# Two-layer streaming encoder on one core: four attention buffers and an even fill, modulation by row products on VectorE, first loads by channel tile

## The chip, the cores and the metric

The kernel runs on one core of one Trainium2 chip. A core has a matrix engine (TensorE, called PE in the profile, with its weight loads as PEld), three elementwise engines (VectorE = DVE, ScalarE = ACT, GpSimd = POOL) and a queue engine (SyncE = SP). SP and ACT start the DMAs. The engines run their own instruction streams in order and meet only at semaphores. The metric is the device time of one execution in microseconds (us), as the median of several runs.

## The reference

The model is a two-layer trunk over 1024 tokens of width 1024, all in fp32. Layer 0 uses forgetting attention (16 heads of 64, causal, with a bias from a cumulative log forget gate), layer 1 a sliding-window attention over a shared K/V. Both have a gated feed-forward part (FFN) with a causal convolution of three taps over 2 x 2816 channels. What the change is about is the modulation: every norm is scaled and shifted, and every branch is gated, by vectors that come from one product of a conditioning vector with a large matrix.

```python
def _modulate(x, g, shift, scale):
    return _rmsnorm(x, g) * (1.0 + scale[:, None, :]) + shift[:, None, :]

c_act = jax.nn.silu(c)                          # 1 x 1024
for l in range(DEPTH):                          # DEPTH = 2
    mod = c_act @ ada_w[l] + ada_b[l]           # 1024 x 6144 per layer
    sh1, sc1, g1, sh2, sc2, g2 = jnp.split(mod, 6, axis=-1)
    if l == N_A:                                # N_A = 1: own product of 1024 x 2048
        k_band, v_band = _shared_kv(x, c_act, kv_norm_g, kv_ada_w, kv_ada_b, kv_w)
    h = _modulate(x, norm1_g[l], sh1, sc1)
    y = forgetting attention (l = 0) or sliding-window attention (l = 1) of h
    x = x + g1[:, None, :] * y
    h = _modulate(x, norm2_g[l], sh2, sc2)
    x = x + g2[:, None, :] * _conv_ffn(h, ...)
return _rmsnorm(x, final_g)
```

In all 112 blocks of 128 modulation values are needed: 16 ahead of the first projection (shift and scale of the first norm), 32 more of layer 0 (the two gates, shift and scale of its second norm), and 64 for layer 1 and the shared K/V.

## The kernel before

Activations lie transposed: channels on the 128 partitions in 8 channel tiles, tokens along the free dimension. Every fp32 product is made of three matmuls with a high part (rounded to fp32r) and a low part (the rest) of each operand; ACT writes the high parts and DVE or POOL subtracts to get the low ones. The weights come through one stream of tiles of 512 KB: SP loads them into two raw buffers (`w_raw`), POOL (and ACT in the FFN) splits them into `w_spl`.

The stages in order of time are these. First X and the modulation weights are loaded, PE sums squares for the norm (line 638), and DVE multiplies each 128 x 512 piece of modulation weights by a scalar per partition and adds it to an accumulator (`ada_steps`, lines 1619 and 1622). PE sums the accumulator over the partitions with one-column matmuls (`ada_cols`, line 631), and DVE adds the bias (line 1633). After the last of these the norm is applied tile by tile: `scaled` on DVE (line 1601), two passes on ACT (lines 1126 and 1129), and `low` on DVE (line 1606); PE makes V and the gate from each tile as it comes (line 664).

Layer 0's attention runs in 4 groups of 4 heads. A head has 12 tasks, each a key block of 128 against up to 512 queries (`TASKS`). In each task slot T of a group PE issues the scores of task T (lines 775, 785, 788), then the value products of task T - `LAG` (lines 810 to 812), then the score maxima for the next head (line 749, counts per slot in `MAX_T`), then steps of the next Q and K projection as filling (line 614, counts per slot in `FILL_1` and `FILL_2`). ACT takes the exponential into `PF` (line 1187) and the high part into `PH` (line 1194), and DVE makes the low part `PL` (line 1726), which the value products wait for. There are three such buffers, and the exponential of a task waits until the value products of the task three before are done. The order of all this is written out by these tables; nothing is scheduled by a tool. Between the tasks DVE also does a modulation step of 128 x 256 in eight of a head's 12 slots, and PE the one-column matmuls in the twelfth.

After the last head PE does the output projection in 8 tiles m (line 614); DVE adds each to X with the gate (line 1833), and the product of tile m waits for the sum of tile m - 2. ACT squares the new X for the next norm.

The FFN (lines 882 for all its matmuls) works on 22 pairs of channel tiles; from the third pair on, the up projection is a seven-product scheme (products A11, A12, S1, S2, S4, A22, S3 of 12 matmuls each) followed by 48 matmuls of the down projection. ACT copies a product out (`u_copy_of`, line 1375), DVE adds such copies (line 1884), makes the convolution taps (lines 1861, 1864) and adds the down projection to X (line 1891). In the 16 pairs 3 to 18 of layer 0 the modulation of layer 1 and of the shared K/V is made beside it: 16 steps of 128 x 256 a pair on DVE from four buffers, with the DMAs issued by ACT between its other work (line 1411), and one-column matmuls on PE after A11 and after S4. The FFN of layer 1 is the same without any modulation.

## Time and profile before

| | |
|---|---|
| median of 3 runs | 2567.02 us (2564.18 to 2570.03) |
| the profiled execution | 2563.79 us |
| its span, first to last instruction | 2562.0 us |
| PE busy | 2371.5 us, 93% of the span, 11208 matmuls |
| DVE / ACT / POOL busy | 1583.9 / 1150.2 / 1133.5 us |
| mean granted TensorE clock | 0.96 of full |
| moved by DMA | 205.41 MB, mean 80 GB/s |

The 1.8 us between the profiled time and its span lie outside the instructions. The profiled execution is 3.2 us under the median of the three runs. PE is busy nearly all the time, but a busy microsecond at half the clock does half the work, so idle time and granted clock are read together, stage by stage.

### The profile page before, as it was taken

The page shows a single profiled execution, that of the slowest core. Times are in us where ns is not written, and L with a number is a line of the kernel's source. Part 1 is how long each engine was busy: PE and PEld are TensorE (multiplying, and loading weights), DVE is VectorE, ACT ScalarE, POOL GpSimd, SP SyncE. Part 2 cuts the span into 40 slices and gives each one's busy share as a digit, 9 for nine tenths or more (in the row PEclk, how much of TensorE's full clock was granted, in tenths as well). Part 3 has the DMA queues.
Part 4 walks back from the last instruction along what each step waited for, and adds up shares of the span by engine and source line. Part 5 has one row for each costly group of instructions (what it writes and reads, how often), then busy time and mean ns, then how long its engine had stood idle before and what let it go on. Part 6 is the DMA issues. An engine that isn't in the chain of part 4 may idle for free.

```text
span 2562.0 us, 31418 instructions
## 1 busy us (share of the span) xinstructions
PE 2371.5 (93%) x11208; PEld 1968.7 (77%) x11208; DVE 1583.9 (62%) x2579; ACT 1150.2 (45%) x1933; POOL 1133.5 (44%) x1568
## 2 busy tenths in 40 slices
PE   5999999898998999999999988987989999999996
PEld 3878788786777878888888877776777888888884
DVE  5575765757428677777775676774285455554446
ACT  4365564646416333333333375663164334333344
POOL 1411312121144666666666443113446666666660
PEclk8999999998899999999999998987999999999998
DMA  6121222223310333433331122114101111112111
GB/s 246 59 91 54 83 83 63 76 65 99 123 46 28 97 116 119 119 119 117 118 121 58 58 99 64 50 42 173 42 28 55 58 50 50 50 50 64 52 58 66
DMA packets 98731, 205.41 MB, mean 80 GB/s; under 512 B 9856, under 2 KB 59648, under 8 KB 98448
## 3 DMA queue, kind: packets, MB, share of 16 engines
q1 hardware_dynamic: 31808, 109.06, 13.5%
q10 hardware_dynamic: 66768, 94.35, 11.7%
q8 instruction: 89, 1.46, 0.2%
q14 instruction: 66, 0.54, 0.1%
HBM read 185.09 MB, written 16.32 MB: 79 GB/s over the span
## 4 chain that ended last, share of the span: by engine, by line
PE 68%; DVE 16%; ACT 7%; DMA 4%; issue 4%; POOL 1%; ACTq 1%; DVEq 0%; SPq 0%; POOLq 0%
PE bank L882 41%; PE bank L614 16%; DVE ada_acc_f L1622 1%; DVE bank L1700 1%; DVE X L1891 1%; PE bank L810 1%; PE bank L749 1%; PE bank L664 1%; DVE PL L1726 1%; PE bank L775 1%; PE bank L785 1%; PE bank L1064 1%; PE bank L811 1%; PE bank L812 1%; DVE ada_acc L1622 1%
## 5 line engine op out<-in xcount | busy, mean ns | idle before, releaser
L882 PE MATMUL bank<-H,w_spl 128*128 128x512 f32 x3744 | 879.4, 393 | 25.3 <-DVE H L1606 14.6
L882 PEld LDWEIGHTS bank<-H,w_spl 128*128 128x128 f32 x3744 | 704.1, 189 | 182.3 <-issue 16.2
L543 POOL TENSOR_TENSOR w_spl<-w_raw,w_spl 128x256 fp32r<-128x256 f32 x688 | 529.3, 796 | 458.5 <-ACT w_spl L1360 457.0
L614 PE MATMUL bank<-H,w_spl 128*128 128x512 f32 x2016 | 506.1, 401 | 25.2 <-DVE H L1606 11.9
L882 PE MATMUL bank<-TB,w_spl 128*128 128x512 f32 x2112 | 494.8, 390 | 0.4 <-ACT sU L1375 0.4
L614 PEld LDWEIGHTS bank<-H,w_spl 128*128 128x128 f32 x2016 | 379.0, 192 | 107.2 <-issue 18.8
L882 PEld LDWEIGHTS bank<-TB,w_spl 128*128 128x128 f32 x2112 | 395.0, 188 | 83.2 <-issue 1.2
L1360 ACT ACTIVATE w_spl<-w_raw 128x512 fp32r<-128x512 f32 x328 | 201.8, 628 | 530.8 <-PE bank L882 369.4
L486 POOL TENSOR_TENSOR pace<-one_s 128x1 f32<-128x1 f32 x50 | 13.3, 267 | 806.7 <-PE bank L775 377.1
L1891 DVE SCALAR_TENSOR_TENSOR X<-bank,mods,X 128x1024 f32<-128x1024 f32 x176 | 225.0, 1278 | 34.4 <-PE bank L882 34.3
L1884 DVE TENSOR_TENSOR bank<-bank,sU 128x512 f32<-128x512 f32 x80 | 55.9, 699 | 269.4 <-PE bank L882 269.3
L550 POOL TENSOR_TENSOR w_raw<-w_raw 128x256 f32<-128x256 f32 x240 | 180.0, 771 | 9.4
L1187 ACT ACTIVATE PF<-bank,negFT 128x512 f32<-128x512 f32 x192 | 111.2, 579 | 155.8 <-PE bank L788 116.9
L493 POOL TENSOR_TENSOR w_spl<-w_raw,w_spl 128x256 fp32r<-128x256 f32 x200 | 170.4, 882 | 4.2
L1622 DVE SCALAR_TENSOR_TENSOR ada_acc_f<-ada_raw_f,c_act,ada_acc_f 128x256 f32<-128x256 f32 x224 | 134.5, 601 | 34.7 <-DMA ada_raw_f<-in_ada_w 17.4
L1700 DVE CUSTOM_DVE_ANT_0 bank<-bank,negF 128x128 f32<-128x128 f32 (+1 forms) x192 | 105.3, 572 | 48.3 <-PE bank L752 29.3
L1375 ACT ACTIVATE sU<-bank 128x512 f32<-128x512 f32 x120 | 71.0, 592 | 127.5 <-PE bank L882 98.7
L1105 ACT ACTIVATE sq<-X 128x1024 f32<-128x1024 f32 x40 | 42.3, 1060 | 190.1 <-DVE X L1833 149.9
L1726 DVE TENSOR_TENSOR PL<-PF,PH 128x512 fp32r<-128x512 f32 x192 | 111.5, 583 | 16.1 <-ACT PH L1194 14.7
L810 PE MATMUL bank<-PH,V 128*128 128x512 f32 x192 | 79.1, 412 | 40.1 <-DVE PL L1726 40.1
L1194 ACT ACTIVATE PH<-PF 128x512 fp32r<-128x512 f32 x192 | 100.8, 525 | 6.1
L1833 DVE SCALAR_TENSOR_TENSOR X<-bank,mods,X 128x1024 f32<-128x1024 f32 x16 | 20.5, 1283 | 127.1 <-PE bank L614 124.6
(179 smaller groups left out, 3310.4 us busy)
## 6 DMA issues: line engine op xcount, KB each, us to landing
w_raw<-in_w_stream SPq DMA_DIRECT2D x184, 512.0 KB, 3.7
ada_raw_f<-in_ada_w ACTq DMA_DIRECT2D x192, 128.0 KB, 2.3
ada_raw_a<-in_ada_w ACTq DMA_DIRECT2D x32, 512.0 KB, 3.9
ada_raw<-in_ada_w SPq DMA_DIRECT2D x8, 1024.0 KB, 14.4
negF<-scratch_f ACTq DMA_DIRECT2D x16, 512.0 KB, 3.8
ada_raw_f<-in_kv_ada_w ACTq DMA_DIRECT2D x64, 128.0 KB, 2.5
X<-in_x_t SPq DMA_DIRECT2D x4, 1024.0 KB, 10.8
X<-in_x_t ACTq DMA_DIRECT2D x4, 1024.0 KB, 8.0
```

Of the source, the lines that this page charges most:

```text
L493: last = pool.tensor_tensor(w_spl[:, u % SPL, 1, q:q + 256], w_raw[:, u % RAW, q:q + 256], w_spl[:, u % SPL, 0, q:q + 256].bitcast(F32), A ...
L543: last = pool.tensor_tensor(block_at(layer, b, 1, q, q + 256), src[:, q:q + 256], block_at(layer, b, 0, q, q + 256).bitcast(F32), ALU.subt ...
L550: last = pool.tensor_tensor(dst[:, q:q + 256], x[:, q:q + 256], y[:, q:q + 256], op)
L614: last = pe.matmul(dst, stat(k, a), mov(k, b), start=(k == 0 and a + b == 0), stop=(k == KT - 1 and a == 1))
L810: pe.matmul(dst, high, PH[slot][:, 0:n], start=(kb == 0), stop=False, skip_group_check=True)
L882: last = pe.matmul(dst, block_at(layer, b, x, k * P, k * P + P), mov(y), start=(start and x + y == 0), stop=(stop and x == 1), skip_group_ ...
L1187: nc.scalar.activation(PF[n_task % 3][:, 0:n], bank(4 + n_task % 2, 0, n), ACT.Exp, bias=negFT[:, kb, h:h + 1]).then_inc(p_exp, 1)
L1360: nc.scalar.activation(block_at(layer, b, 0), src, ACT.Copy).then_inc(b_hi, 1)
L1622: V_.scalar_tensor_tensor(acc, raw(k), c_act[:, k:k + 1], acc, ALU.mult, ALU.add).then_inc(steps, 1)
L1700: V_.tensor_tensor_reduce(bank(c % 2, 0, n), bank(c % 2, 0, n), negF[:, h % 2, k0:k0 + n], 1.0, NEG, ALU.add, ALU.max, mx[h % 2][:, i + 4 ...
L1726: V_.tensor_tensor(PL[n_task % 3][:, 0:n], PF[n_task % 3][:, 0:n], PH[n_task % 3][:, 0:n].bitcast(F32), ALU.subtract).then_inc(p_lo, 1)
L1891: V_.scalar_tensor_tensor(X[:, m], pair(4 + 2 * (m % 2)), mods[:, gc + m:gc + m + 1], X[:, m], ALU.mult, ALU.add).then_inc(dn_ev, 1)
```

## The change

Three things change.

1. **Attention.** The buffers `PH`, `PF` and `PL` become four (`NP = 4`) and the value products follow three tasks behind the scores (`LAG = 3`). The filling of groups 1 to 3 is two steps in each of 16 slots, where it was three and two by turns in 13. The maxima of a group's third head are spread over eight slots in place of six. DVE takes the low parts of Q and K a slot later. The maxima wait for the parts of Q and K that they read, not for all of them.
2. **Modulation.** The weights come transposed (`ada_t`), so that a row of 1024 products belongs to one output channel, and the activated conditioning vector is spread over all partitions (`cb0`, `cbO`, `cbF`). One fused multiply-and-sum on DVE (`row_dot`, an instruction on the row and one that reads the sum out) gives a block of 128 values with its bias. The accumulators, the one-column matmuls on PE and their evictions are gone. The first 16 blocks are made ahead of the first projection; the next 32 lie beside the output projection instead of beside the attention (4 rows ahead of the sum of each tile, loaded by ACT in pieces of 2 MB into two buffers); the last 64 stay in the FFN's pairs 3 to 18, as 128 half rows of 512, eight a pair, loaded in pieces of 256 KB into two buffers. The conditioning vector (4 KB before) is loaded as 512 KB and its activated form goes through a scratch tensor in DRAM.
3. **First loads.** SP loads X ahead of the first two weight tiles. The modulation weights arrive by channel tile, shift and scale together, and DVE makes the norm of each tile as soon as its two rows are multiplied.

```diff
-LAG = 2
+LAG = 3
+NP = 4
...
-MAX_T = [[2, 1, 1, 1, 1, 1, 1, 2, 2, 0, 0, 0], [0, 0, 0, 2, 2, 2, 2, 2, 2, 0, 0, 0]]
+MAX_T = [[2, 1, 1, 1, 1, 1, 1, 2, 2, 0, 0, 0], [0, 0, 2, 1, 2, 1, 2, 1, 2, 1, 0, 0]]
...
-FILL_1 = [3, 2, 3, 2, 3, 2, 3, 2, 3, 2, 3, 2, 2]
+FILL_1 = [2] * 16
...
-            load(0, 0, None)
-            load(1, 1, None)
             for j in range(4):
                 sp.dma_start(X[:, 2 * j:2 * j + 2], x_t.rearrange("k p s -> p k s")[
                     :, 2 * j:2 * j + 2]).then_inc(x_in[j], 16)
+            load(0, 0, None)
+            load(1, 1, None)
+            for kt in range(KT):
+                sp.dma_start(ada_raw0[:, kt], ada_t.rearrange("b p k -> p b k")[:, kt:kt + 9:8]).then_inc(ada0_in[kt], 16)
...
+                if h and c in (0, 8):
+                    pe.wait_ge(qk_lo, 8 if h == 1 else 2 * (4 * (h // 2) + (2 if c == 0 else 3)) + e + 1)
...
-                        pe.wait_ge(qk_lo, 2 * (4 * (h // 2) + 4))
...
-                    if t == 11:
-                        ada_cols(ada_acc_a, 2, 8 * (4 * g + hl + 1), 1, 0)
...
-                        if layer == 0 and name == "A11" and p in ADA_PAIRS[1:] + [ADA_PAIRS[-1] + 1]:
-                            ada(2 * (p - ADA_PAIRS[0]) - 1, p)
-                        if layer == 0 and name == "S4" and p in ADA_PAIRS:
-                            ada(2 * (p - ADA_PAIRS[0]), p)
...
-            act.dma_start(c_s[:], c_t).then_inc(c_in, 16)
+            act.dma_start(cb0[:], c_row[0:1, :].partition_broadcast(P)[:, 0, :]).then_inc(c_in, 16)
...
-            nc.scalar.activation(c_act[:], c_s[:], ACT.Silu).then_inc(cact_done, 1)
+            nc.scalar.activation(cb0[:], cb0[:], ACT.Silu).then_inc(cact_done, 1)
+            act.wait_ge(cact_done, 1)
+            act.dma_start(dC, cb0[0:1, :]).then_inc(c_out, 16)
...
+            def load_ada(m):
+                if m < 8:
+                    if m >= 2:
+                        act.wait_ge(ada_step, ADA_1 + 4 * (m - 1))
+                    act.dma_start(ada_raw_o[:, m % 2], ada_t.rearrange("b p k -> p b k")[:, M_G1 + m:M_G2 + m + 1:8]
+                                  ).then_inc(adao_in[m % 2], 16)
...
-                if n_task >= 3:
-                    act.wait_ge(pv_ps, n_task - 2)
-                nc.scalar.activation(PF[n_task % 3][:, 0:n], bank(4 + n_task % 2, 0, n), ACT.Exp,
+                if n_task >= NP:
+                    act.wait_ge(pv_ps, n_task - NP + 1)
+                nc.scalar.activation(PF[n_task % NP][:, 0:n], bank(4 + n_task % 2, 0, n), ACT.Exp,
...
-                    if t == 4:
-                        act.wait_ge(ada_step, 8 * (4 * g + hl) + 4)
-                        load_ada(4 * g + hl, 1)
-                    if t == 10 and 4 * g + hl + 1 < 4 * NG:
-                        act.wait_ge(ada_step, 8 * (4 * g + hl + 1))
-                        load_ada(4 * g + hl + 1, 0)
...
+            act.wait_ge(pv_ps, NT * NH)
+            act.dma_start(cbO[:], dC[0:1, :].partition_broadcast(P)[:, 0, :]).then_inc(cbo_in, 16)
+            load_ada(0)
+            load_ada(1)
+            for m in range(7):
+                squares(1)(m)
+                load_ada(m + 2)
...
+                    if layer == 0 and j < 128:
+                        b, half = M_L1 + j % 64, j // 64
+                        if j >= 2:
+                            act.wait_ge(ada_step, ADA_2 + j - 1)
+                        if j == 64:
+                            act.wait_ge(ada_step, ADA_2 + 64)
+                        if j % 64 == 0:
+                            act.dma_start(cbF[:], dC[0:1, half * HALF:half * HALF + HALF].partition_broadcast(P)[:, 0, :]
+                                          ).then_inc(cbf_in, 16)
+                        act.dma_start(ada_raw_f[:, j % 2], ada_t[b, :, half * HALF:half * HALF + HALF]
+                                      ).then_inc(adaf_in[j % 2], 16)
...
+                    def load(i):
+                        if ADA_PAIRS[0] <= p <= ADA_PAIRS[-1] + 1:
+                            load_ada(8 * (p - ADA_PAIRS[0]) + i + 2)
...
+            def row_dot(raw, cb, begin, col):
+                V_.tensor_tensor_reduce(raw, raw, cb, 1.0, begin, ALU.mult, ALU.add, col).then_inc(ada_step, 1)
+            def mod_row(raw, cb, b):
+                row_dot(raw, cb, modb[:, b:b + 1], mods[:, b:b + 1])
...
+            def first_mods(kt):
+                dve.wait_ge(ada0_in[kt], 16)
+                for i in range(2):
+                    mod_row(ada_raw0[:, kt, i], cb0[:], KT * i + kt)
+                dve.wait_ge(ada_step, 2 * kt + 2)
+                V_.scalar_tensor_tensor(coef[:, kt:kt + 1], mods[:, M_SC1 + kt:M_SC1 + kt + 1], 1.0,
+                                        gain[:, G_N1 + kt:G_N1 + kt + 1], ALU.add, ALU.mult)
+            for k in range(KT + 1):
+                if k < KT:
+                    first_mods(k)
+                    if k == 0:
+                        dve.wait_ge(rs_done, 1)
+                    scaled(0, k, h_hi)
+                if k == 0:
+                    dve.wait_ge(const_r, 1)
+                    V_.tensor_tensor(wvg[:, :, 1, 256:272], wf_raw[:], wvg[:, :, 0, 256:272].bitcast(F32),
+                                     ALU.subtract).then_inc(vg_in, 1)
+                if k:
+                    low(0, k - 1)
...
+            def mods_of_tile(m):
+                dve.wait_ge(adao_in[m % 2], 16 * (m // 2 + 1))
+                if m == 0:
+                    dve.wait_ge(cbo_in, 16)
+                for i in range(4):
+                    mod_row(ada_raw_o[:, m % 2, i], cbO[:], M_G1 + KT * i + m)
...
-                    if t in (0, 1, 2, 3, 6, 7, 8, 9):
-                        ada_one(4 * g + hl, t - 2 * (t >= 6))
-                    for n in qk_done(g, T):
+                    for n in qk_done(g, T - 1) if T else []:
                         qk_low(n, 0)
-                    for n in qk_done(g, T - 1) if T else []:
+                    for n in qk_done(g, T - 2) if T > 1 else []:
...
+                        mods_of_tile(m)
+                        dve.wait_ge(ada_step, ADA_1 + 4 * m + 1)
...
+                def mod_half(j):
+                    b, half = M_L1 + j % 64, j // 64
+                    dve.wait_ge(adaf_in[j % 2], 16 * (j // 2 + 1))
+                    if j % 64 == 0:
+                        dve.wait_ge(cbf_in, 16 * (half + 1))
+                    first = mods_a[:, j % 64:j % 64 + 1]
+                    row_dot(ada_raw_f[:, j % 2], cbF[:], first if half else modb[:, b:b + 1], mods[:, b:b + 1] if half else first)
...
+                    def step(i):
+                        if with_ada:
+                            mod_half(8 * (p - ADA_PAIRS[0]) + i)
```

The order of instructions shows it at three places. The first is on DVE near the program's start, before: the end of the modulation and the first tiles of the norm.

```order
L1622 SCALAR_TENSOR_TENSOR ada_acc_88<-ada_raw_50,c_act,ada_acc_88 128x512 [waits ada0_step,ada0_in7]
L1622 SCALAR_TENSOR_TENSOR ada_acc_88<-ada_raw_50,c_act,ada_acc_88 128x512 [waits ada0_step] x3
L1633 TENSOR_TENSOR mods<-bank,modb 128x4 [waits ada_ps] x2
L1593 SCALAR_TENSOR_TENSOR coef<-mods,gain 128x8 [waits ada_ev]
L1649 TENSOR_TENSOR wvg<-wf_raw,wvg 128x8x16 [waits const_r]
L1601 TENSOR_TENSOR tn<-X,rstd 128x1024 [waits rs_done]
L1601 TENSOR_TENSOR tn<-X,rstd 128x1024
L1606 TENSOR_TENSOR H<-hf,H 128x1024 [waits h_hi]
L1601 TENSOR_TENSOR tn<-X,rstd 128x1024 [waits h_hi]
L1606 TENSOR_TENSOR H<-hf,H 128x1024 [waits h_hi]
```

The same place after the change; `ada_raw_50` holds the weight rows, `cb_51` the conditioning vector, and an ISA row is the fused multiply-and-sum or its read-out.

```order
L1632 SCALAR_TENSOR_TENSOR coef<-mods,gain 128x1 [waits ada_step]
L1597 TENSOR_TENSOR tn<-X,rstd 128x1024 [waits rs_done]
L1643 TENSOR_TENSOR wvg<-wf_raw,wvg 128x8x16 [waits const_r]
L1613 ISA ada_raw_50,mods<-ada_raw_50,cb_51,modb 128x1024 [waits ada0_in1]
L1613 ISA mods 128x1
L1613 ISA ada_raw_50,mods<-ada_raw_50,cb_51,modb 128x1024
L1613 ISA mods 128x1
L1632 SCALAR_TENSOR_TENSOR coef<-mods,gain 128x1 [waits ada_step]
L1597 TENSOR_TENSOR tn<-X,rstd 128x1024
L1602 TENSOR_TENSOR H<-hf,H 128x1024 [waits h_hi]
```

The passes on the norm now lie between row products, where they followed the last of them.

The second is on PE in the third head's turn of a group in attention, before: three slots with scores (`QS`, `QM`), value products (`PH`, `PL`) and maxima (`KS_59`).

```order
L775 MATMUL bank<-QS_54,KS_58 128x384 [waits p_exp]
L785 MATMUL bank<-QM_56,KL_60 128x384
L788 MATMUL bank<-id_r,mask_r 128x128
L810 MATMUL bank<-PH_65,V 128x512 [waits p_lo]
L811 MATMUL bank<-PH_65,V 128x512
L812 MATMUL bank<-PL_71,V 128x512
L775 MATMUL bank<-QS_54,KS_58 128x256 [waits p_exp]
L785 MATMUL bank<-QM_56,KL_60 128x256
L788 MATMUL bank<-id_r,mask_r 128x128
L810 MATMUL bank<-PH_66,V 128x512 [waits p_lo]
L811 MATMUL bank<-PH_66,V 128x512
L812 MATMUL bank<-PL_72,V 128x512
```

After the change, the slots with the same score tasks:

```order
L770 MATMUL bank<-QS_55,KS_59 128x384 [waits p_exp]
L780 MATMUL bank<-QM_57,KL_61 128x384
L783 MATMUL bank<-id_r,mask_r 128x128
L805 MATMUL bank<-PH_67,V 128x512 [waits p_lo]
L806 MATMUL bank<-PH_67,V 128x512
L807 MATMUL bank<-PL_75,V 128x512
L744 MATMUL bank<-KS_60,QS_56 128x512 [waits s_read]
L747 MATMUL bank<-mask_r,id_r 128x128
L770 MATMUL bank<-QS_55,KS_59 128x256 [waits p_exp]
L780 MATMUL bank<-QM_57,KL_61 128x256
L783 MATMUL bank<-id_r,mask_r 128x128
L805 MATMUL bank<-PH_68,V 128x512 [waits p_lo]
```

In the slots with 384 and 256 score columns the value products still have 512 columns in both, but they are those of one task earlier, and one maximum stands in the piece, which came earlier before.

The third is on DVE in a pair of the first FFN, before: the modulation steps (`ada_acc_f`) between the taps, the sums and the down projection's sums into X.

```order
L1622 SCALAR_TENSOR_TENSOR ada_acc_f<-ada_raw_f,c_act,ada_acc_f 128x256 [waits ada_step,adaf_in1]
L1861 SCALAR_TENSOR_TENSOR cG<-bank,conv_s,cG 128x1023 [waits cv0]
L1864 SCALAR_TENSOR_TENSOR cG<-bank,conv_s,cG 128x1022 [waits cv1]
L1622 SCALAR_TENSOR_TENSOR ada_acc_f<-ada_raw_f,c_act,ada_acc_f 128x256 [waits ada_step,adaf_in2]
L1622 SCALAR_TENSOR_TENSOR ada_acc_f<-ada_raw_f,c_act,ada_acc_f 128x256 [waits ada_step,adaf_in3]
L1884 TENSOR_TENSOR bank<-bank,s_104 128x512 [waits u_copy,up_ps]
L1882 TENSOR_TENSOR bank<-sU,bank 128x512 [waits u_copy,up_ps]
L1622 SCALAR_TENSOR_TENSOR ada_acc_f<-ada_raw_f,c_act,ada_acc_f 128x256 [waits ada_step,adaf_in0]
L1891 SCALAR_TENSOR_TENSOR X<-bank,mods,X 128x1024 [waits dn_ev,dn_ps]
L1861 SCALAR_TENSOR_TENSOR cV<-bank,conv_s,cV 128x1023 [waits cv0]
L1864 SCALAR_TENSOR_TENSOR cV<-bank,conv_s,cV 128x1022 [waits cv1]
L1891 SCALAR_TENSOR_TENSOR X<-bank,mods,X 128x1024 [waits dn_ev,dn_ps]
```

After the change the same stretch has half as many modulation rows, each with its read-out, and they take two buffers by turns.

```order
L1613 ISA ada_raw_f,mods_a<-ada_raw_f,cbF,modb 128x512 [waits adaf_in1]
L1613 ISA mods_a 128x1
L1850 SCALAR_TENSOR_TENSOR cG<-bank,conv_s,cG 128x1023 [waits cv0]
L1853 SCALAR_TENSOR_TENSOR cG<-bank,conv_s,cG 128x1022 [waits cv1]
L1613 ISA ada_raw_f,mods_a<-ada_raw_f,cbF,modb 128x512 [waits adaf_in0]
L1613 ISA mods_a 128x1
L1873 TENSOR_TENSOR bank<-bank,s_107 128x512 [waits u_copy,up_ps]
L1871 TENSOR_TENSOR bank<-sU,bank 128x512 [waits u_copy,up_ps]
L1613 ISA ada_raw_f,mods_a<-ada_raw_f,cbF,modb 128x512 [waits adaf_in1]
L1613 ISA mods_a 128x1
L1880 SCALAR_TENSOR_TENSOR X<-bank,mods,X 128x1024 [waits dn_ev,dn_ps]
L1850 SCALAR_TENSOR_TENSOR cV<-bank,conv_s,cV 128x1023 [waits cv0]
```

## Rows read from the trace of the kernel before

**Rows 1.** Windows by attention group: us, busy of engines, clock, DMA, GB/s.

```profile
...
81.00:262.00 181.00, 165.50 (x895) 141.58 (x896) 113.20 (x276) 93.52 (x177) 48.20 (x77) 0.97 0.22 69
262.00:406.00 144.00, 132.44 (x743) 114.39 (x742) 92.85 (x227) 81.92 (x152) 32.24 (x54) 0.99 0.24 74
406.00:556.00 150.00, 139.11 (x777) 120.54 (x776) 95.56 (x230) 82.11 (x153) 32.25 (x54) 0.97 0.23 71
556.00:672.00 116.00, 100.22 (x453) 83.11 (x452) 83.36 (x191) 75.67 (x135) 20.45 (x36) 0.85 0.32 100
...
```

**Rows 2.** Waits of TensorE, window 81 to 672: us in total, times, longest.

```profile
...
PE bank L810 <- DVE PL L1726: 40.1, 30, 3.5
...
```

**Rows 3.** The same view, window 556 to 672.

```profile
...
PE bank L810 <- DVE PL L1726: 14.6, 11, 2.8
...
```

**Rows 4.** Timeline from 340 to 352: start, us, engine, line, operation.

```profile
...
343.14 0.69 DVE L1726 TENSOR_TENSOR PL<-PF,PH 128x512 fp32r<-128x512 f32 x1
...
343.89 0.49 PE L810 MATMUL bank<-PH,V 128*128 128x512 f32 x1 [0.66 <-DVE PL L1726]
...
```

**Rows 5.** Windows of the four stretches with a lowered clock.

```profile
...
148.00:163.00 15.00, 11.46 (x51) 10.37 (x51) 10.94 (x24) 9.13 (x20) 2.30 (x4) 0.66 0.31 107
300.00:320.00 20.00, 15.96 (x77) 13.04 (x75) 16.81 (x43) 15.32 (x28) 5.52 (x9) 0.91 0.22 66
450.00:480.00 30.00, 26.45 (x123) 22.19 (x124) 25.05 (x67) 18.80 (x36) 2.49 (x3) 0.83 0.26 79
600.00:672.00 72.00, 59.54 (x246) 49.02 (x247) 54.41 (x128) 48.05 (x84) 0.03 (x1) 0.76 0.33 106
...
```

**Rows 6.** Windows 81 to 672, line 631 alone: TensorE and its loads.

```profile
...
81.00:672.00 591.00, 9.06 (x64) 11.01 (x64) 0.95 0.25 77
...
```

**Rows 7.** Timeline of the first stage.

```profile
...
33.16 1.06 ACT L1114 ACTIVATE rstd<-rstd 128x1024 f32<-128x1024 f32 x1
...
54.46 25.92 PE L664 MATMUL bank<-wvg,H 128*128 128x272 f32 x192 [5.55 <-DVE H L1606]
55.36 1.22 DVE L1606 TENSOR_TENSOR H<-hf,H 128x1024 fp32r<-128x1024 f32 x1
55.48 1.24 ACT L1126 ACTIVATE hf<-tn,mods,coef 128x1024 f32<-128x1024 f32 x1 [0.16 <-DVE tn L1601]
...
```

**Rows 8.** VectorE groups by form: busy us, mean ns, idle before.

```profile
...
L1700 DVE CUSTOM_DVE_ANT_0 bank<-bank,negF 128x512 f32<-128x512 f32 x96 | 66.9, 708 | 24.5 <-PE bank L749 17.4 <-PE bank L752 6.7
...
L1700 DVE DVE_READ_ACCUMULATOR2_ANT mx<- 128x1 f32 x192 | 26.9, 140 | 0.0
...
L1622 DVE SCALAR_TENSOR_TENSOR ada_acc<-ada_raw,c_act,ada_acc 128x512 f32<-128x512 f32 x28 | 21.7, 777 | 1.3
...
L1700 DVE CUSTOM_DVE_ANT_0 bank<-bank,negF 128x128 f32<-128x128 f32 x32 | 9.5, 295 | 13.5 <-PE bank L752 13.1 <-DMA negF<-scratch_f 0.5
...
```

**Rows 9.** DMA from 669 to 690: GB/s in 40 slices; size, us to landing.

```profile
...
GB/s 0 0 0 109 109 335 445 414 414 406 421 421 421 406 437 421 406 429 406 398 437 398 414 343 0 0 0 0 0 0 0 0 0 0 0 70 125 250 398 187
...
X<-in_x_t ACTq DMA_DIRECT2D x4, 1024.0 KB, 8.0
...
```

**Rows 10.** Timeline of VectorE in the output projection.

```profile
...
681.91 1.28 DVE L1833 SCALAR_TENSOR_TENSOR X<-bank,mods,X 128x1024 f32<-128x1024 f32 x1 [5.42 <-PE bank L614]
...
692.79 1.28 DVE L1833 SCALAR_TENSOR_TENSOR X<-bank,mods,X 128x1024 f32<-128x1024 f32 x1 [9.60 <-PE bank L614]
...
```

**Rows 11.** Timeline of TensorE in the first FFN: the fifth product, S4.

```profile
...
864.53 2.88 PE L882 MATMUL bank<-H,w_spl 128*128 128x512 f32 x12
...
1370.73 2.88 PE L882 MATMUL bank<-H,w_spl 128*128 128x512 f32 x12
...
1400.68 2.88 PE L882 MATMUL bank<-H,w_spl 128*128 128x512 f32 x12
...
```

**Rows 12.** Waits of the page's whole span.

```profile
...
ACT sU L1375 <- DVE ada_acc_f L1622: 28.9, 9, 3.4
...
```

**Rows 13.** Section 6 of the page: DMA issues, KB each, us to landing.

```profile
...
ada_raw_f<-in_ada_w ACTq DMA_DIRECT2D x192, 128.0 KB, 2.3
...
```

220 lines of the change are left out of this document (70 added, 150 removed).

## The prediction

> **What bounds the kernel now.** I read the windows first, one for each attention group, because a busy share over the whole span mixes stages. From 81 to 672 TensorE is busy for 165.5 + 132.4 + 139.1 + 100.2 = 537.3 of 591 us, so it stands still for 53.7 us, and the last group's granted clock is 0.85 [rows 1]. No other engine is full there: in the second group DVE has 92.9 and ACT 81.9 of 144 us. So attention is bound by TensorE with short waits, not by a full engine. The waits of TensorE say for what: 40.1 us in 30 waits for `PL`, the low part that DVE makes, in front of the value products [rows 2]; 14.6 us of it fall in the last group [rows 3]. The timeline shows one: DVE ends `PL` at 343.83 and the value product starts at 343.89, 0.66 us late [rows 4]. The longest is 3.5 us. Then I looked for stretches with a lowered clock. There are four, and (1 - clock) x length is 5.1 + 1.8 + 5.1 + 17.3 = 29.3 us [rows 5]; DVE has 10.9 of 15 and 16.8 of 20 us in the first two, and TensorE is idle for 3.5 and 4.0. In the first FFN TensorE hardly waits, so what counts is what it issues: the fifth product comes every (1370.73 - 864.53) / 16 = 31.64 us in the 16 pairs with modulation, and after 29.95 us in the first pair without [rows 11].
>
> **First stage.** Removed are the accumulator steps behind which the norm waited. The norm's factor is ready at 33.16 + 1.06 = 34.2, yet V starts at 54.46 and ends at 80.38 [rows 7]. Now DVE alternates. No row shows a fused multiply-and-sum of 1024 columns from SBUF. The same instruction takes 0.295 us with 128 columns and 0.708 with 512, thus 1.076 ns a column, and the read-out takes 0.14 [rows 8]: 1.26 + 0.14 = 1.40 us a row. The bounds are 1.22 us, what a plain subtraction of 1024 columns takes [rows 7], and 2 x 0.777 + 0.14 = 1.69 us, from the fp32 step with two SBUF operands, whose mean over 28 is 0.777 us at 512 columns [rows 8]. I take 1.40, since it is the same kind of instruction.
> ACT's first load grows from 4 KB to 512 KB; at some 410 GB/s [rows 9] that is 1.3 us ahead of the constants and of the squares: the factor comes at 35.5. From there: norm of tile 0 1.2, gate weights 0.3, then seven turns of two rows (2.8), a coefficient of a few columns (no row has its kind: 0.3, an estimate from twice the 0.14 of the smallest row above, once for itself and once for its wait), norm and low part (2 x 1.2 [rows 7]) = 5.5 us each, 38.5 in all: 75.5. That is the end of tile 6; the norm of tile 7 was done 1.2 ahead of it, and two ACT passes of 1.24 and the low part of 1.2 follow: 78.0. TensorE needs 25.92 / 8 = 3.2 us a tile, fewer than 5.5, so only the last tile is left to it: 81.2 at full clock, 84.4 if that tile runs at half. Against 80.4 before this is +0.8 to +4.0. Passes that follow each other on DVE overlap a little, which takes back up to a microsecond or two. I take **+1 us**, with -1 to +7 (the dear bound is 14 rows x 0.29 = 4 us more).
>
> **Attention.** Three parts.
> The one-column matmuls go: 64 of them are busy for 9.1 us [rows 6], -9.
> A fourth buffer and one task more of lag give the chain of exponential, high part and low part another slot, some 144 / 48 = 3.0 us in the second group [rows 1]. That covers the waits (1.3 us in the mean, 3.5 at most [rows 2]) wherever DVE is late only because a subtraction, a normalisation and a maximum fell together. It can't cover those where DVE or ACT is full for many slots. The last group's second half has no filling: in 600 to 672 DVE is busy for 54.4 and ACT for 48.1 of 72 us [rows 5]. Of the 40.1 us I let 10 stay, most of it there. DVE loses 8 modulation steps a head too, which speaks for this. -30.
> The clock: where the waits go, so should the dips behind them. The first three dips are 12.0 us, the last 17.3 [rows 5]. I credit -9: most of the first three and nothing of the last, since there TensorE stays short of work.
> Together **-48 us**. The bounds are -9 (only the matmuls) and -83 (all 53.7 idle and all 29.3 of clock). The evened filling takes work out of early slots and puts it into slots 13 to 15, where a wait stood; I cost it within this sum. The part of K that a maximum in slot 14 reads is now taken in DVE's slot 13, and TensorE's slot is a slot and a half behind by then: covered, at most 2 us a group if not.
> In front of `PL` DVE's queue holds now one slot more, and the maxima wait for DVE as before; the exponential of task T waits for the value products of T - 4, which TensorE issues in slot T - 1, as it issued those of T - 3 before.
>
> **Output projection.** DVE now makes four rows ahead of each sum: 4 x 1.40 + 1.28 [rows 10] + 1.22 for the squares = 8.1 us against a tile's 692.79 - 681.91 = 10.88 us on TensorE, in which it waited 9.60 [rows 10]. That is hidden, from the second tile on. The first isn't: the rows come on ACT's queue behind X. X was done at about 681.5 (4 MB, landing 8.0 us after issue [rows 9]); 0.5 and 2 MB more at 410 GB/s are 6.1 us, and the landing: 688.5. Four rows end at 694.1, the sum at 695.4, and tile 2, which waits for it, would have started at 692.8: **+2.5 us**. Later loads of 2 MB take 5 to 6 us and are issued a tile ahead. Bounds 0 and +12, the latter if each row took 1.69 us and each load shared its queue with the weights.
>
> **First FFN.** Per pair 8 one-column matmuls and their waits go. (31.64 - 29.95) x 16 = 27.0 us is what they cost [rows 11]. DVE's part: 8 x (0.71 + 0.14) = 6.8 us a pair [rows 8], fewer than the 16 steps of 128 x 256 before. The risk is the two buffers: a load waits for the step two before it, and lands 2.3 us after issue in the case of 128 KB [rows 13]. ACT's queue holds copies that TensorE waits for behind such a load; these were delayed before as well (28.9 us in 9 waits [rows 12]) without showing in TensorE's time. I keep 1 us: **-26 us**, bounds -27 and -10.
>
> **Sum.** 1 - 48 + 2.5 - 26 = -70.5. The profiled execution took 2563.8 us (span 2562.0 and 1.8 around it), so 2493.3; it lies 3.2 us under the median of the runs, which gives **2496 us**. The stages behind the first FFN run as before.
>
> **A rule against it.** The rows show no halving: the step with two fp32 operands from SBUF took 0.777 us for 512 columns [rows 8], not far over a nanosecond and a half a column. The Trainium skill, Vector Engine (DVE) Microarchitecture Reference, section "Points that are easy to get wrong", says that a multiply-and-sum of this family with two SBUF sources that aren't bf16 runs at half throughput, since no read port is left for the accumulator. By that rule a row takes the time of rival B and the sum is 2519 us, by the row it is 2496; the trace can't decide it, since the maxima of rows 8 read one operand from PSUM.
>
> **Rivals.**
> A. *Attention is full, not late.* DVE at 83.4 and ACT at 75.7 of 116 us in the last group [rows 1] speak for it, and so does DVE with 16.8 of 20 us from 300 on [rows 5]. Against it: 30 waits of 1.3 us in the mean, apart from each other [rows 2]. Then the lag gives 10 and the clock nothing: -19 in place of -48, 2525 us.
> B. *A row product runs at half rate*, about 2 x 1.1 + 0.2 = 2.4 us for 1024 columns. No row has this operand pattern with an accumulator; the 0.777 speaks against. The first stage gets 14 more microseconds (14 rows x 1.0), a tile of the output projection takes 4 x 2.4 + 2.5 = 12.1 against 10.9, 9 us in 7 tiles, and the FFN's 8 x 1.25 still fit: 2496 + 23 = 2519 us. The Trainium skill's rule of the section above gives this time.
> C. *Two buffers are too few in the FFN.* A step waits for its landing in every pair, a sum comes late and TensorE waits 1 us in each of 16: 2512 us.
> D. *The waits and the dips go wholly*, last group too: the 10 us that I let stay, and 12 of the last dip's 17.3: 2474 us.
> E. *The clock falls* (the other side). The evener filling leaves no slot of the third head dense, and TensorE's clock stays at the lower of its levels (1.2 of 2.4 GHz) for long stretches, as it did after the waits at 148 to 163 and in 600 to 672 [rows 5]. Attention's mean clock is 0.95 [rows 6]. Its 537 us of work stretch by 537 x (0.95 / c - 1); at c = 0.84 this is 70 us and eats the whole gain, so below that the kernel is slower; at 0.80 it is 101 us, 2597 us. Against it: two steps of filling are in every slot up to 15, and waits that lowered the clock go.
>
> **How the numbers follow.** The forecast has 0.60, A 0.17, B 0.07, C 0.06, D 0.05, E 0.05. The forecast's own range, from the smaller bounds of the attention term, is 2478 to 2514. The range is 2474 to 2533: it takes in A with some slack, B, C and D, and leaves out E and the ends. Under 0.2% (5 us) this kernel's runs can't tell a change from none. All cases but E lie under 2562, thus faster 0.94; same 0.02 and slower 0.04, from E on both sides of its point.
>
> **What would show it.** Value products should wait for `PL` for 10 us or less in attention, and the first three dips should be gone; if the waits stay near 40, A holds. The row product's mean should be 1.25 us with a read-out of 0.14; over 2 us is B. V should end near 80 to 82. TensorE should stand still once, for 2 to 3 us, ahead of the third tile of the output projection. The fifth product should come every 30.0 us; 31 or more is C. The second half of the program should take what it took.

## The result, and the profile after

The changed kernel takes 2521.3 us (median of 4 runs, 2520.0 to 2527.0) against 2565.9 us for the kernel before beside it (4 runs, 2564.2 to 2570.0): a ratio of 0.983, 95% interval 0.981 to 0.985. That is 44.6 us less. The forecast was 70 us less, 2496; its range of 2474 to 2533 holds the time, its own narrower range of 2478 to 2514 does not. The profiled execution has a span of 2520.5 us, 41.5 under the span before.

I cut both spans at the same places of the program, each read from TensorE's timeline: the end of V's matmuls, the first matmul of the output projection, the first of the FFN, and the FFN's last. The times of single stages come from one profiled execution of each kernel. Kernels whose attention is the same instruction for instruction had it last 543.8, 545.1, 546.7 and 547.9 us, so a difference of under some 4 us there says nothing.

| stage, us | before | after | change | forecast |
|---|---|---|---|---|
| start to end of V | 80.4 | 80.7 | +0.3 | +1 |
| from there to the output projection | 590.3 | 549.0 | -41.3 | -48 |
| output projection to FFN | 102.5 | 104.1 | +1.6 | +2.5 |
| first FFN | 698.7 | 693.2 | -5.5 | -26 |
| everything behind | 1090.1 | 1093.5 | +3.4 | 0 |

One stage is far off, the first FFN, and attention is off by 7 us. The attention groups after the change stand here as those of before do in [rows 1]; each line is a stretch, its length, the busy time of TensorE, its weight loads, DVE, ACT and POOL, the granted clock, the DMA share and GB/s.

```profile
81.00:262.00 181.00, 169.04 (x902) 144.00 (x903) 102.80 (x251) 96.35 (x182) 50.05 (x84) 0.96 0.16 48
262.00:390.00 128.00, 122.47 (x688) 105.36 (x687) 76.77 (x183) 78.42 (x146) 26.67 (x48) 1.00 0.16 48
390.00:520.00 130.00, 124.73 (x699) 107.30 (x698) 78.51 (x180) 80.94 (x150) 29.87 (x54) 1.00 0.17 49
520.00:629.67 109.67, 97.33 (x510) 81.48 (x509) 75.96 (x172) 77.06 (x138) 19.31 (x36) 0.95 0.23 72
```

The second group took 144 us and takes 128; the last had a clock of 0.85 and has 0.95. TensorE's idle time fell from 53.7 to 35.1 us. What it waits for has changed its name. TensorE's waits from 83 to 629.67 (us in total, times, longest), to be held against [rows 2]:

```profile
PE bank L744 <- DVE mx L1694: 12.8, 23, 1.4
PE bank L770 <- DVE QM L1712: 10.7, 7, 2.5
PE bank L754 <- DVE nmx L1706: 3.5, 6, 0.9
PE bank L805 <- DVE PL L1720: 2.6, 3, 1.6
PE bank L618 <- DVE V L1655: 2.0, 1, 2.0
PE bank L770 <- ACT PF L1175: 1.7, 2, 0.9
```

The 40.1 us for `PL` in 30 waits are 2.6 us in 3. But the waits for the maxima of the next head's scores (`mx`), for the rows made of them (`QM`) and for their negatives (`nmx`) were 8.9 us before (7.6 for `mx`, 1.3 for `QM`) and are 27.0 now.

In the first FFN the fifth product, S4, stood 31.64 us apart [rows 11]. After the change, in TensorE's timeline, two neighbouring pairs with modulation and two with the last of them:

```profile
825.13 2.88 PE L875 MATMUL bank<-H,w_spl 128*128 128x512 f32 x12
856.34 2.88 PE L875 MATMUL bank<-H,w_spl 128*128 128x512 f32 x12
...
1325.85 2.88 PE L875 MATMUL bank<-H,w_spl 128*128 128x512 f32 x12
1355.82 2.88 PE L875 MATMUL bank<-H,w_spl 128*128 128x512 f32 x12
```

A pair with modulation mostly lasts 31.21 us (31.3 in the mean of the 16), one without 29.97. Of the 1.7 us that each pair was to lose, 0.4 went. TensorE's waits in the stage (733.8 to 1427.04) name the reason:

```profile
PE bank L875 <- DVE X L1880: 12.0, 18, 0.9
PE bank L875 <- DVE H L1602: 7.3, 1, 7.3
```

The second is the norm ahead of the stage, there before as well. The first is the sum of the down projection into X; before the change it was 4.9 us in 12 waits. The timeline of one pair shows it:

```profile
1056.07 1.11 DVE L1613 CUSTOM_DVE_ANT_0 ada_raw_f<-ada_raw_f,cbF,modb 128x512 f32<-128x512 f32 x1
1057.12 0.08 DVE L1613 DVE_READ_ACCUMULATOR2_ANT mods_a<- 128x1 f32 x1
1057.12 1.27 DVE L1880 SCALAR_TENSOR_TENSOR X<-bank,mods,X 128x1024 f32<-128x1024 f32 x1
1058.32 1.27 DVE L1850 SCALAR_TENSOR_TENSOR cV<-bank,conv_s,cV 128x1023 f32<-128x1023 f32 x1
1058.44 2.63 PEld L875 LDWEIGHTS bank<-H,w_spl 128*128 128x128 f32 x12 [0.47 <-DVE X L1880]
1059.62 1.28 DVE L1853 SCALAR_TENSOR_TENSOR cV<-bank,conv_s,cV 128x1022 f32<-128x1022 f32 x1
1060.82 1.28 DVE L1880 SCALAR_TENSOR_TENSOR X<-bank,mods,X 128x1024 f32<-128x1024 f32 x1
...
1062.15 2.14 PE L875 MATMUL bank<-H,w_spl 128*128 128x512 f32 x8 [0.65 <-DVE X L1880]
```

One row product of 1.11 us stands directly ahead of a sum into X that frees the accumulators which TensorE's third output tile takes; two taps later the sum for the fourth is late too. This was the theory to test: the order on DVE, and neither the number of buffers nor the landing of the loads.

### The profile page after: what moved, and what is told of

Its sections match the earlier page's. It is cut to its first block, busy times and chain, and to the rows that moved or that the text cites. A ratio compares the mean times of both kernels' runs of the same rounds, so it can differ in the third digit from the quotient of the medians.

```text
span 2520.5 us, 30443 instructions
## 1 busy us (share of the span) xinstructions
PE 2340.4 (93%) x10984; PEld 1933.7 (77%) x10984; DVE 1535.0 (61%) x2470; ACT 1149.8 (46%) x1933; POOL 1170.3 (46%) x1580
## 3 DMA queue, kind: packets, MB, share of 16 engines
q10 hardware_dynamic: 36098, 95.91, 11.7%
## 4 chain that ended last, share of the span: by engine, by line
PE 67%; DVE 14%; ACT 8%; issue 4%; POOL 4%; DMA 3%; ACTq 1%; DVEq 0%; POOLq 0%
PE bank L875 40%; PE bank L618 17%; DVE X L1880 2%; POOL w_spl L547 1%; PE bank L634 1%; POOL w_raw L554 1%; DVE H L1602 1%; PE bank L744 1%; PE bank L770 1%; PE bank L780 1%; PE bank L805 1%; PE bank L807 1%; PE bank L806 1%; DVE tn L1597 1%; POOL S3f L554 1%
## 5 line engine op out<-in xcount | busy, mean ns | idle before, releaser
L875 PEld LDWEIGHTS bank<-H,w_spl 128*128 128x128 f32 x3744 | 705.5, 189 | 195.6 <-DVE X L1880 26.8
L547 POOL TENSOR_TENSOR w_spl<-w_raw,w_spl 128x256 fp32r<-128x256 f32 x688 | 544.0, 818 | 445.0 <-ACT w_spl L1350 443.6
L618 PE MATMUL bank<-H,w_spl 128*128 128x512 f32 x2016 | 517.5, 407 | 24.7 <-DVE H L1602 10.8
L618 PEld LDWEIGHTS bank<-H,w_spl 128*128 128x128 f32 x2016 | 386.1, 196 | 108.9 <-issue 20.5
L485 POOL TENSOR_TENSOR pace<-one_s 128x1 f32<-128x1 f32 x50 | 14.2, 283 | 740.6 <-PE bank L770 358.5
L1880 DVE SCALAR_TENSOR_TENSOR X<-bank,mods,X 128x1024 f32<-128x1024 f32 x176 | 225.0, 1278 | 34.5 <-PE bank L875 34.4
L492 POOL TENSOR_TENSOR w_spl<-w_raw,w_spl 128x256 fp32r<-128x256 f32 x200 | 180.3, 932 | 4.2
L1175 ACT ACTIVATE PF<-bank,negFT 128x512 f32<-128x512 f32 x192 | 111.1, 578 | 113.0 <-PE bank L783 80.7
L1694 DVE CUSTOM_DVE_ANT_0 bank<-bank,negF 128x128 f32<-128x128 f32 (+1 forms) x192 | 105.5, 572 | 76.2 <-PE bank L747 47.7
L487 POOL TENSOR_SCALAR w_spl<-w_raw 128x256 fp32r<-128x256 f32 x200 | 98.7, 522 | 0.0
L1850 DVE SCALAR_TENSOR_TENSOR cG<-bank,conv_s,cG 128x1023 f32<-128x1023 f32 x44 | 56.4, 1283 | 48.2 <-ACT cG L1375 48.2
L770 PE MATMUL bank<-QS,KS 128*128 128x512 f32 x192 | 69.5, 362 | 12.9 <-DVE QM L1712 10.7
## 6 DMA issues: line engine op xcount, KB each, us to landing
X<-in_x_t SPq DMA_DIRECT2D x4, 1024.0 KB, 11.1
```

The costliest lines, as they stand in the source:

```text
L487: last = pool.tensor_scalar(w_spl[:, u % SPL, 0, q:q + 256], w_raw[:, u % RAW, q:q + 256], 1.0, 1.0, ALU.mult, ALU.mult)
L492: last = pool.tensor_tensor(w_spl[:, u % SPL, 1, q:q + 256], w_raw[:, u % RAW, q:q + 256], w_spl[:, u % SPL, 0, q:q + 256].bitcast(F32), A ...
L547: last = pool.tensor_tensor(block_at(layer, b, 1, q, q + 256), src[:, q:q + 256], block_at(layer, b, 0, q, q + 256).bitcast(F32), ALU.subt ...
L618: last = pe.matmul(dst, stat(k, a), mov(k, b), start=(k == 0 and a + b == 0), stop=(k == KT - 1 and a == 1))
L875: last = pe.matmul(dst, block_at(layer, b, x, k * P, k * P + P), mov(y), start=(start and x + y == 0), stop=(stop and x == 1), skip_group_ ...
L1175: nc.scalar.activation(PF[n_task % NP][:, 0:n], bank(4 + n_task % 2, 0, n), ACT.Exp, bias=negFT[:, kb, h:h + 1]).then_inc(p_exp, 1)
```

## The experiments

All start from the changed kernel. Each was timed in 3 rounds beside the kernel before, which took 2564.6 to 2565.6 us in all three groups of runs; the one on the output projection, which is not in the table, ran once. "Attention" is the time from 83 us to the first matmul of the output projection.

| kernel | time, us | ratio, 95% interval | attention, us | first FFN, us |
|---|---|---|---|---|
| before | 2565.9 | 1 | 587.7 | 698.7 |
| changed | 2521.3 | 0.983 [0.981, 0.985] | 546.7 | 693.2 |
| sixth product moved | 2505.8 | 0.977 [0.975, 0.979] | 545.1 | 680.2 |
| no loads in the FFN | 2519.7 | 0.982 [0.980, 0.984] | 547.9 | 691.7 |
| old lag and fill, 4 buffers | 2531.6 | 0.987 [0.985, 0.989] | 557.2 | 692.8 |
| modulation alone | 2531.5 | 0.986 [0.985, 0.988] | 557.5 | 692.2 |
| old lag, new fill | 2531.3 | 0.987 [0.985, 0.988] | 554.4 | 692.8 |
| new lag, old fill | 2523.9 | 0.984 [0.982, 0.986] | 551.5 | 692.9 |
| modulation alone, DVE loaded | 2545.8 | 0.992 [0.990, 0.994] | 568.2 | 694.5 |
| maxima a task earlier | 2518.8 | 0.982 [0.980, 0.984] | 545.5 | 692.6 |
| both edits | 2504.9 | 0.976 [0.975, 0.978] | 546.3 | 679.0 |
| both, QM ahead of PL | 2499.2 | 0.974 [0.973, 0.976] | 537.6 | 678.8 |
| both, QM ahead of O_st | 2500.9 | 0.975 [0.973, 0.977] | 539.1 | 680.4 |

**The FFN's order.**

```diff
                     sum_of(p, 6, 4, 2, ALU.subtract, sU)
                     if p == PAIRS - 1:
                         low_part(FT // 2 - 1, 0)
-                    else:
-                        step(5)
                     half_residual(p, 0)
                     taps(p, 1, pair(2))
                     half_residual(p, 1)
+                    step(5)
                     step(6)
```

> The sixth modulation product of each pair moves from directly ahead of the residual sums of output tiles 0 and 1 to behind the second of them; nothing else changes. Theory (order on VectorE): after the change a pair with products lasts 31.2 us in the first FFN and one without 30.0, because the product of about 1.05 us stands in VectorE's order ahead of the sums that TensorE's third and fourth output tile wait for (about 0.5 and 0.7 us of waiting per pair, 16 pairs). Then the period falls to 30.0 to 30.3, TensorE's waits for VectorE X fall from about 12 us in 18 to under 4, the first FFN from 693.2 us to 674 to 679, and the time to 2502 to 2508. Rival (landing: VectorE is held by its own waits for ada_raw_f, 44 us in 25, and falls behind whatever the order): the period stays 31.0 to 31.3 and the time 2517 to 2524. Second rival (VectorE is simply full with eight products a pair): the wait moves to another sum, the period stays over 30.8.

2505.8 us, 15.5 less than the changed kernel, and the intervals don't meet. In the same stretch of a pair the two sums into X no longer have a product ahead of them, and TensorE's wait is 0.28 us:

```profile
866.62 1.28 DVE L1880 SCALAR_TENSOR_TENSOR X<-bank,mods,X 128x1024 f32<-128x1024 f32 x1
867.99 1.28 DVE L1850 SCALAR_TENSOR_TENSOR cV<-bank,conv_s,cV 128x1023 f32<-128x1023 f32 x1
869.31 1.28 DVE L1853 SCALAR_TENSOR_TENSOR cV<-bank,conv_s,cV 128x1022 f32<-128x1022 f32 x1
870.51 1.28 DVE L1880 SCALAR_TENSOR_TENSOR X<-bank,mods,X 128x1024 f32<-128x1024 f32 x1
871.70 0.74 DVE L1613 CUSTOM_DVE_ANT_0 ada_raw_f<-ada_raw_f,cbF,modb 128x512 f32<-128x512 f32 x1
...
871.84 0.50 PE L875 MATMUL bank<-H,w_spl 128*128 128x512 f32 x1 [0.28 <-DVE X L1880]
```

The stage fell by 13.0 us to 680.2; I had expected 674 to 679. TensorE's waits for X are 4.4 us in 9 over the stage, from 12.0 in 18. The period reads 30.3 to 30.5 us in most pairs and over 30.7 in four. So the order was the cause of most, and about half a microsecond a pair over the 29.97 without modulation is left that I did not settle.

**The loads.**

```diff
-                    if layer == 0 and j < 128:
+                    if layer == 0 and j < 2:
...
-                    dve.wait_ge(adaf_in[j % 2], 16 * (j // 2 + 1))
+                    if j < 2:
+                        dve.wait_ge(adaf_in[j], 16)
+                    else:
+                        dve.wait_ge(ada_step, ADA_2 + j - 1)
...
```

> In the first FFN only the first two rows of modulation weights are loaded; the 128 products run all the same, in place and over the same two buffers again (against a row of small weights in place of c), so the modulation that they give is left out. The order on VectorE stays as after the change. Theory (order on VectorE): the sixth product still stands ahead of the two residual sums, so the period of a pair stays 31.0 to 31.3 us and the time 2515 to 2523. Rival (landing of the rows, two buffers): with no row to wait for, the period falls to 30.0 to 30.3 and the time to 2500 to 2508. If the loads' own traffic and ScalarE's part in issuing them mattered, the time would lie between, and ScalarE's waits for VectorE's steps (ada_step) would be gone with it.

No change: 2519.7 us, the intervals lie over each other. DVE no longer waits for `ada_raw_f` at all (44.5 us in 25 waits between 820 and 1360 after the change), and the period is 31.20 to 31.24 us in all 16 pairs. A landing for which DVE waits 1.8 us in the mean cost TensorE nothing here: two buffers are enough.

**What the modulation's leaving gave attention.** The first kernel puts lag, fill and maxima back and keeps the fourth buffer; the second takes the buffer away too.

```diff
-LAG = 3
+LAG = 2
-MAX_T = [[2, 1, 1, 1, 1, 1, 1, 2, 2, 0, 0, 0], [0, 0, 2, 1, 2, 1, 2, 1, 2, 1, 0, 0]]
+MAX_T = [[2, 1, 1, 1, 1, 1, 1, 2, 2, 0, 0, 0], [0, 0, 0, 2, 2, 2, 2, 2, 2, 0, 0, 0]]
-FILL_1 = [2] * 16
+FILL_1 = [3, 2, 3, 2, 3, 2, 3, 2, 3, 2, 3, 2, 2]
...
-                        if t == 8 + hl % 2:
+                        if t == 8:
```

> The lag between scores and value products, the fill table and the table of maxima are as before the change; the fourth buffer is there but the lag never asks for more than three, and the modulation columns are off TensorE. So it shows what the modulation part alone does to the attention. Theory as in the prediction (about 9 us of one-column matmuls and a part of the 9 us of the clock come from this part, 30 us of waits from buffers and fill): attention, 546.7 us after the change and 588.0 before, then lasts 570 to 580 us and the time is 2545 to 2555. Rival (the fill of one-column matmuls itself made the waits for PL, or the waits come from VectorE's order and not from the lag): attention falls under 560 us, the time to 2530 or less.

My theory fell: without the new lag, fill and maxima 30 us of attention went, where I had expected 8 to 18.

```diff
-NP = 4
+NP = 3
```

(on top of the diff above)

> The modulation part alone: lag, number of buffers, fill table and table of maxima all as before the change. With four buffers and the old lag the attention ended at 640.2, against 670.7 before and 629.7 after the change, so a fourth buffer (the exponentials then wait for the value products of four tasks back and not three) or the modulation leaving gave 30 of the 41 us. Theory (modulation: TensorE has 9 us of one-column matmuls fewer, VectorE some 90 instructions fewer, and the clock dips go): attention ends at 640 to 645 and the time is 2530 to 2537. Rival (buffers): it ends at 652 to 662, the time 2543 to 2555.

2531.5 us, the same as with the buffer. The fourth buffer does nothing with the old lag, which never asks for it, and the rest of the change brings 33 us (against the kernel before beside it) of the 44.6. "Modulation alone" is a short name. Against the kernel before, this one also keeps some small moves of the change: DVE takes the low parts of Q and K a slot later, the output is normalised a slot later, and the maxima wait only for the parts of Q and K that they read. No run took these back, so how much of the 33 us is theirs is not shown. TensorE's attention before, for this kernel, and after the change (windows from 83 to the output projection of each):

```profile
83.00:670.72 587.72, 534.69 (x2852) 457.49 (x2851) 383.06 (x919) 331.18 (x608) 131.23 (x216) 0.95 0.25 77
```

```profile
83.00:640.50 557.50, 516.48 (x2793) 437.16 (x2791) 328.25 (x776) 330.84 (x611) 124.46 (x217) 0.98 0.17 52
```

```profile
83.00:629.67 546.67, 513.23 (x2792) 437.83 (x2791) 332.08 (x776) 331.56 (x612) 123.97 (x217) 0.98 0.18 53
```

Busy time fell by 18.2 us and idle time by 12.0 (53.0 to 41.0) when the modulation left; lag and fill took 3.3 and 7.6 more. The waits for `PL` are 26.8 us here. To see which half of the modulation was which, I put DVE's part back as empty work, without the matmuls:

```diff
                     behind(g, T)
+                    if t in (0, 1, 2, 3, 6, 7, 8, 9):
+                        dve.wait_ge(ex, 8 * (4 * g + hl) + t - 2 * (t >= 6) + 1)
+                        V_.scalar_tensor_tensor(extra[:], extra[:], one_s[:, 0:1], extra[:], ALU.mult,
+                                                ALU.add).then_inc(ex, 1)
...
```

> The kernel with the modulation part alone, and in it 128 extra instructions of 128x256 on VectorE (multiply and add into a scratch tile, none of them needed) at the eight tasks of each head where the kernel before had its modulation steps; TensorE's one-column matmuls stay out. Theory (the 12 us of idle time of TensorE that the modulation took with it were VectorE's steps in the way of PL): attention ends at 650 to 656, against 640.5, with PL waits back at 36 to 42 us, and the time is 2541 to 2547. Rival (it was the one-column matmuls and the clock that they cost): attention ends at 640 to 645, the time 2531 to 2536. What is left to 670.7 is then the matmuls and the clock, 18 us by TensorE's busy time.

2545.8 us, 14.3 more, with attention at 568.2; the 128 instructions on DVE cost 10.7 us in attention. The waits for `PL` came back from 26.8 to 31.4 us only, under the 36 to 42 that I gave:

```profile
PE bank L807 <- DVE PL L1723: 31.4, 31, 3.2
```

DVE was not full in either kernel (388 of 568 us and 328 of 558). That its instructions cost by where they stood is therefore likely, but no run moved them. The remaining 19.5 us of attention, 587.7 to 568.2, are 14.2 us of TensorE's busy time (534.7 to 520.5) and 5.3 of its idle time (53.0 to 47.7). The one-column matmuls (9.1 us busy before [rows 6]), the clock, the loads of the weights and the small moves named above are all in it; they were not parted.

**Lag and fill.**

```diff
-LAG = 3
+LAG = 2
```

> The changed kernel with a lag of two tasks between score and value product in place of three; four buffers and the new fill and maxima stay. Old lag and old fill together ended the attention at 640.2 (PL waits 27 us). Theory (the lag is what removes the PL waits): PL waits stay at 25 to 35 us, attention ends at 638 to 645, the time is 2529 to 2538. Rival (the even fill removes them): PL waits under 12 us, attention ends at 630 to 634 and the time is 2520 to 2526.

The waits for `PL` are 26.3 us, and the whole 10 us are lost: 2531.3, as with nothing of the attention part. The converse keeps the lag and takes the old tables (the diff of the tables above, without that of `LAG`):

> The changed kernel with its four buffers and the lag of three, but the fill table and the table of maxima as before the change. So far: modulation alone 2531.5 us, lag undone but new fill 2531.3, all 2521.3. Theory (the lag is worth the 10 us; the fill alone did nothing): TensorE's waits for PL stay under 6 us, attention ends at 629 to 633, and the time is 2520 to 2525. Rival (lag and even fill are only worth something together): attention ends at 636 to 641, the time 2527 to 2533. If the new table of maxima is what brought the waits for maxima and QM (27 us), they fall under 18 us here.

Attention is 4.8 us longer than after the change, the time 2.6 us with intervals that overlap: the lag brings nearly all, the even fill at most a little. A lag of three with only three buffers was not run, so lag and fourth buffer count as one part. The table of maxima isn't the source of the new waits: `mx` 11.1, `QM` 11.3, `nmx` 1.8 us with the old one, 24.2 against 27.0, not under 18. They come with the lag: with a lag of two and the new tables they were 7.3, 3.1 and 1.7, which is 12.1 us.

**The waits that came in place of PL.**

```diff
-..., [0, 0, 2, 1, 2, 1, 2, 1, 2, 1, 0, 0]]
+..., [0, 0, 2, 2, 1, 2, 1, 2, 2, 0, 0, 0]]
...
-                        if t == 8 + hl % 2:
+                        if t == 8:
```

> For the heads hl = 0, 2 before hl = 1's scores the maxima of head 1 are taken earlier and negated in task 8 rather than 9, as for the other heads. Theory: the changed attention waits at the end of each second head for chunk maxima and rows (maxima <-mx, value products <-nmx, scores <-QM: 12.8, 3.5 and 10.7 us in all), since the maxima of that head are now spread by twos to the ninth task; taken one task earlier, the QM and nmx waits there (about 1.7 us in each of four groups) go and the time falls by 4 to 9 us, to 2512 to 2517. Rival (the mx waits are of VectorE's whole load there, not of the order): the maxima are asked for earlier, wait more, and the time stays within 3 us of the changed kernel (2518 to 2524) or rises by up to 5.

2518.8 us, which can't be told from 2521.3. `mx` fell to 9.1 and `nmx` to 1.7, but `QM` stayed (11.7) and the exponentials rose from 1.7 to 4.4. The timeline of this kernel at the end of a second head shows what `QM` stands behind:

```profile
310.66 0.69 DVE L1730 TENSOR_TENSOR O_st<-bank,rec 64x512 f32<-64x512 f32 x1
311.39 0.56 DVE L1720 TENSOR_TENSOR PL<-PF,PH 128x384 fp32r<-128x384 f32 x1
311.98 1.22 DVE L1712 TENSOR_TENSOR QM<-bank,sel 16x1024 fp32r<-16x1024 f32 x1
313.23 0.63 DVE L1720 TENSOR_TENSOR PL<-PF,PH 128x256 fp32r<-128x256 f32 x2
...
313.25 0.50 PE L770 MATMUL bank<-QS,KS 128*128 128x512 f32 x1 [1.54 <-DVE QM L1712]
```

The transposed maxima are in PSUM at 310.7 and `QM` itself takes 1.22 us; an `O_st` and a `PL` that no one asks for yet go first. The next three kernels carry this edit and the FFN's together.

> Both edits of the two kernels before together: the sixth product of a pair behind the residual sum of tile 1, and head 1's maxima a task earlier. The first gave about 15 us, the second 1 to 3. Theory (the gains add): attention ends near 628.4 as with the maxima alone, the first FFN lasts about 678 us, the time 2501 to 2507. Rival (the 2 us of the maxima were scatter): 2504 to 2508, no different from the first edit alone.

2504.9 us: 0.9 less than the FFN's edit alone, inside the scatter.

```diff
+                    if hl < 3 and t == 10:
+                        max_rows(4 * g + hl + 1)
                     if T:
                         low_task(g, T - 1)
...
-                        if t == 10:
-                            max_rows(4 * g + hl + 1)
```

> As the kernel with both edits, and in the eleventh task of a head VectorE takes the rows of maxima (QM, 1.2 us) ahead of the low part PL of the task before instead of behind it. Theory: the wait of TensorE's first score of the next head for QM (1.5 us at each third head, 11.7 us in all, with the maxima a task earlier) is the length of what VectorE does ahead of QM, a PL of 0.56 us among it, and PL is asked for only three tasks later; so QM is ready 0.5 to 0.6 us earlier for twelve heads, the QM waits fall to 4 to 8 us and the time to 2496 to 2503. Rival (PL becomes late in turn, with the lag of three tasks not enough for 1.2 us more): PL waits rise by as much, and the time stays at 2501 to 2508.

2499.2 us, the fastest: 5.7 under both edits (in attention 8.7), 22 under the changed kernel and 65 under the one before. The wait above became 0.94 us, `QM` in all 8.4, and TensorE's clock in attention is 0.99. The interval, 0.973 to 0.976, overlaps that of both edits at its edge only.

```diff
-                    if hl < 3 and t == 10:
-                        max_rows(4 * g + hl + 1)
...
+                    if hl < 3 and t == 9:
+                        max_rows(4 * g + hl + 1)
                     behind(g, T)
```

> The kernel with both edits, and VectorE takes QM one task earlier than in the kernel with QM ahead of PL: ahead of the normalized output O_st (0.7 us) too. Theory: QM then starts with the transposed maxima, 0.65 us earlier; the QM waits fall from 8.4 us to 3 to 6, and the time from 2499.2 to 2494 to 2498. Rival (the QM waits that are left come at a few heads, and VectorE now stands still for the transpose and gives it back in PL and maxima): no change, 2498 to 2502.

The rival holds: 2500.9 us, inside the 2498 to 2502 that I gave it. TensorE's waits from 83 to 622 in this kernel:

```profile
PE bank L744 <- DVE mx L1694: 8.7, 18, 1.3
PE bank L805 <- DVE PL L1720: 8.5, 11, 1.6
PE bank L770 <- ACT PF L1175: 4.6, 7, 0.9
PE bank L770 <- DVE QM L1712: 3.0, 7, 1.3
```

`QM` lost 5.4 us and `PL` gained 4.6. The step before had given time; this one only renames the wait.

**The output projection.**

```diff
-                for i in range(4):
-                    mod_row(ada_raw_o[:, m % 2, i], cbO[:], M_G1 + KT * i + m)
+                for i in range(4):
+                    c = M_G1 + KT * i + m
+                    V_.tensor_copy(mods[:, c:c + 1], modb[:, c:c + 1]).then_inc(ada_step, 1)
```

> The changed kernel without the 32 row products beside the output projection (a copy of one column stands for each; the loads of the rows are there still, so the gates and the FFN's modulation of layer 0 lack their products). Theory (TensorE waited 1.4 us for the first tile's sum, and for nothing else there): TensorE's wait for X at line 1822 goes, and the stage from 629.7 to the FFN's first matmul, 104.1 us, is 102 to 104. Rival (the row products held up the squares and the norm behind the projection as well, or the load of 2 MB a tile slows the weights): under 101 us, or no change at all above 104.

2519.5 us in its one run. TensorE's wait for X is gone, yet the stage takes 104.2 us, as after the change: between my theory (102 to 104) and its rival this decides nothing. Two more readings bear on it. The first: summed over the whole stage, (1 - clock) x length is 4.3 us before, 4.2 after and 5.8 here, while TensorE's idle time is 9.8, 11.2 and 9.9. So after the change the wait fills most of the 1.6 us, and in this run a lower clock does. The second: the output projection is the same in eleven other kernels here, and in each of them TensorE waits 2.3 to 3.6 us for the first tile's sum. The trace after the change and that of the modulation alone:

```profile
PE bank L618 <- DVE X L1822: 1.4, 1, 1.4
PE bank L618 <- DVE X L1822: 3.6, 1, 3.6
```

The first two tiles took 23.64 us on TensorE in the trace after the change, and 22.0 in that of the modulation alone; what those two tiles took longer no longer had to be waited for. In all twelve kernels the third tile starts 24.9 to 25.6 us into the stage, where the first two need 22.0. The stage lasts 104.1 to 107.9 us in the twelve, with a median of 105.8, so the changed kernel's trace is the shortest of them.

## Why the prediction was right and wrong

**First stage, +1: right.** +0.3 us. V's matmuls now follow the norm tile by tile; the last two tiles run from 74.38 to 80.70, after a wait of 1.59 us. DVE's row product with 1024 columns takes 1.28 us at its shortest with a read-out of 0.08, against 1.26 + 0.14 forecast:

```profile
648.31 1.28 DVE L1613 CUSTOM_DVE_ANT_0 ada_raw_o<-ada_raw_o,cbO,modb 128x1024 f32<-128x1024 f32 x1 [13.85 <-DMA ada_raw_o<-in_ada_t]
649.52 0.08 DVE L1613 DVE_READ_ACCUMULATOR2_ANT mods<- 128x1 f32 x1
```

This decides against rival B's 2.4 us. The Trainium skill, Vector Engine (DVE) Microarchitecture Reference, section "Points that are easy to get wrong", says that an instruction of the shape `S2S2D2_STT` with two SBUF sources that aren't bf16 halves its throughput. No run shows whether the row product has that shape; its two sources are fp32 in SBUF and it took 1.25 ns a column at its shortest, less than the 1.5 of the step with two such sources and no sum [rows 8], and not the 2.4 us a row of rival B, so no halving shows.

**Attention, -48: right in size within 7 us, and in part by luck.** The matmuls' 9 us are gone, as forecast, though no run here shows them by themselves. For the clock I credited 9 us and nothing of the last dip. Summed over stretches of 10 us, (1 - clock) x length from 83 us to the output projection fell from 29.0 to 11.9, and the last dip fell with the others: 600 to 630 has 0.83, where 600 to 672 had 0.76 over more than twice the length [rows 5]. Of the first three dips the second and third are gone (a clock of 1.00 in both), the first is not: 0.77 from 148 to 163, where it was 0.66. Nearly all of this came when the modulation left, since the sum is 10.2 us in that kernel. For the waits I took -30, with the extra slot as the main cause. The waits for `PL` did fall, by 37.5 us, but 18.1 came back as waits for maxima and rows, and idle time fell by 19.6. Of that 12.0 went with the modulation, which I had named only as speaking for the sum, and 7.6 with lag and fill. Busy time fell by 21.5, where matmuls and clock were to bring 18. The slot of lag is worth 8 us of attention (554.4 to 546.7) and 10 of the time, which is what rival A gave it. A's time, 2525 us, is nearer to the 2521 measured than mine, but by luck too: it had attention at -19, where -41 was measured, since it gave nothing to DVE's fewer steps and to the clock, and the FFN at -26. The step of mine that failed is "the maxima wait for DVE as before": with the slot of lag these waits rose from 8.9 to 27.0 us.

**Output projection, +2.5: right, and somewhat short.** +1.6 us in the trace after the change, +3.3 by the median of the twelve traces, against one trace of before. The mechanism is as forecast: the first four rows began 13.85 us after DVE was free for them, 18.6 us into the stage (17.8 forecast); the sum into X ended at 654.53, 24.9 us into it (24.7 forecast); and TensorE waited once, ahead of the third tile, from 653.3 to 654.7. That its wait was 1.4 us and not 3 comes of the longer first two tiles in this one execution (granted clock 0.93 there, 1.00 in the trace of the modulation alone), as said above. The granted clock of the whole stage is 0.96 before and after.

**First FFN, -26: wrong.** -5.5. The step that failed is the last of it, "I keep 1 us", which counted DVE's work (eight products in place of sixteen steps) and not where each stands. (The products themselves were dearer too: 0.90 + 0.08 us in the mean against 0.71 + 0.14, thus 7.8 us a pair and not 6.8.) Rival C had the size, 1 us of waiting a pair, and the wrong cause: it blamed the two buffers, and without any landing the period did not move by 0.1 us. The sign that I had named for it, a fifth product every 31 us or more, came true without the cause. Moving one product gave 13.0 us of the stage and 15.5 of the time. With it the FFN is at -18.5; what keeps the rest from -26 is not settled.

**The sum.** The FFN is 20.5 us of the 29 between the spans' change and the forecast, attention 6.7, and the stages behind the first FFN, held at nothing, 3.4. These are 1.5 us in the kernel with the product moved and 2.8 in the fastest, and between -1.6 and +4.9 over the changed kernels here, which are the same there, so I do not explain them. The range held because 2474 to 2533 was wide. The narrower one, 2478 to 2514, failed; the prediction does not show how its ends come from the bounds of the attention term.

## What to carry to other kernels

Before costing work that "fits beside" another engine, write down which instruction stands directly ahead of each one that the bound engine waits for: here one product of 0.7 to 1.1 us at the wrong place cost 0.8 us in each of 16 pairs, while a late load on an engine with time to spare cost nothing. When a buffer takes a wait away, look at the next thing that the same engine delivers, since half of the 37 us came back under another name. And change one part at a time: fourth buffer, lag, fill and moved modulation arrived together, and nearly all of attention's gain came with the modulation and the lag. Even "modulation alone" carried small moves with it that no run took back.

## What the runs showed of the hardware

The row product of 1024 columns has different lengths, by what POOL does beside it. The timeline of the output projection, DVE and POOL:

```profile
662.37 3.48 POOL L492 TENSOR_TENSOR w_spl<-w_raw,w_spl 128x256 fp32r<-128x256 f32 x2
663.49 1.76 DVE L1613 CUSTOM_DVE_ANT_0 ada_raw_o<-ada_raw_o,cbO,modb 128x1024 f32<-128x1024 f32 x1
...
666.86 1.27 DVE L1613 CUSTOM_DVE_ANT_0 ada_raw_o<-ada_raw_o,cbO,modb 128x1024 f32<-128x1024 f32 x1
666.95 2.56 POOL L487 TENSOR_SCALAR w_spl<-w_raw 128x256 fp32r<-128x256 f32 x4
```

Wholly beside POOL's two-operand subtraction it takes 1.74 to 1.76 us, with POOL idle 1.27 to 1.28, and beside POOL's one-operand copy 1.27 to 1.41 (those at 657.05 and 658.40 took 1.4). One product, at 662.28, took 1.28 although a subtraction ran beside it, and I do not know why. POOL is slowed as well: four copies of 128x256 took 1.52 us with DVE idle (from 642.96) and 4.49 beside it (from 655.94); its subtraction of 128x256 takes 3.48 / 2 = 1.74 us here, and the same one took 2.84 / 4 = 0.71 us while DVE stood still:

```profile
644.56 2.84 POOL L492 TENSOR_TENSOR w_spl<-w_raw,w_spl 128x256 fp32r<-128x256 f32 x4
```

The mean of the 32 products in the output projection is 1.58 us, that of the 128 products of 512 columns in the FFN 0.90, against 0.74 at its shortest. And an edit that shortens waits can bring more through the clock than through the waits: from the kernel with both edits to the one with `QM` ahead of `PL`, TensorE's idle time in attention fell by 2.8 us (32.9 to 30.1) and its busy time by 5.9 (513.4 to 507.5), while the sum of (1 - clock) x length went from 10.2 to 3.0 us. It is not in proportion: with the modulation alone the idle time was 41.0 us and that sum already 10.2, and four traces with the changed kernel's attention read 8.3 to 11.9.
